# Twenty-eight weight tiles of a hybrid decoder layer multiplied by seven block products for eight, in a stage of their own ahead of attention

## The reference, cut to what matters

```python
mod = silu(c) @ w_ada + b_ada                      # shift, scale, gate
h = rmsnorm(x, norm_w) * (1 + scale) + shift       # 1024 tokens x 1024 channels
aq, ak, av, az, mq, mk, mv, mo, mz, mi, mf, ga, gm = split(h @ w_in)
att = sliding_window_attention(rope(aq), rope(ak), av, sinks)
y_att = (att * silu(az)) @ w_att
mq = silu(causal_conv(mq)); mk = silu(causal_conv(mk)) * d ** -0.5
hm = mlstm_chunkwise(mq, mk, mv, mi + b_i, log_sigmoid(mf + b_f))   # 4 heads of 256
hm = hm * rsqrt(mean(hm * hm) + eps) * m_norm_w * sigmoid(mo)
y_m = (hm * silu(mz)) @ w_m
merged = sigmoid(ga) * y_att + sigmoid(gm) * y_m
out = rmsnorm(x + gate * (merged @ w_out), final_norm_w)
```

## Time and profile before

| | |
|---|---|
| time, median of 3 runs | 1346.77 us (1345.74 to 1346.91) |
| profiled execution, first to last instruction (its span; the profile states no other time of it) | 1343.5 us |
| PE busy | 1308.8 us, 97% |
| DVE, ACT, POOL busy | 644.1, 427.4, 609.3 us |
| chain that ended last | PE 92%, DVE 4%, ACT 2% |
| moved by DMA | 89.44 MB, mean 67 GB/s |

### The profile page before, as it was taken

One profiled execution on the slowest core, in us unless ns is written; L12 is line 12 of the kernel. 1 busy time (PEld: TensorE's weight loads), 2 busy tenths in 40 slices (PEclk: granted clock), 3 DMA queues, 4 the chain that ended last, 5 costly groups with the idle time before them and its releaser, 6 DMA issues.

```text
span 1343.5 us, 20127 instructions
## 1 busy us (share of the span) xinstructions
PE 1308.8 (97%) x6941; PEld 1112.3 (83%) x6941; DVE 644.1 (48%) x1343; ACT 427.4 (32%) x1065; POOL 609.3 (45%) x824
## 2 busy tenths in 40 slices
PE   4899999999999999999999999999999999999997
PEld 3687988889788888889888988898889888788886
DVE  5776775857750000354554355435544421544335
ACT  5556564554630000133313332323232211311111
POOL 3507052160634444592665176517660555567240
PEclk9899999999999999999999999999999999999999
DMA  9702011020211310420410041004100133331602
GB/s 327 194 17 64 17 48 33 1 63 0 56 49 54 94 48 30 126 64 1 110 47 16 0 109 47 16 0 119 53 16 16 47 110 94 110 94 47 204 26 100
DMA packets 124951, 89.44 MB, mean 67 GB/s; under 512 B 12370, under 2 KB 117986, under 8 KB 124899
## 3 DMA queue, kind: packets, MB, share of 16 engines
q1 hardware_dynamic: 121056, 76.09, 20.2%
q10 hardware_dynamic: 3842, 12.68, 2.8%
HBM read 80.36 MB, written 8.41 MB: 66 GB/s over the span
## 4 chain that ended last, share of the span: by engine, by line
PE 92%; DVE 4%; ACT 2%; issue 1%; DMA 1%; ACTq 0%; POOL 0%; DVEq 0%
PE pp L574 27%; PE pp L575 26%; PE pp L576 26%; PE pp L742 2%; PE pp L853 2%; PE pp L725 1%; PE pp L726 1%; PE pp L733 1%; PE pp L662 1%; PE pp L845 1%; PE pp L710 1%; DVE prob_t L1485 1%; PE pp L648 1%; DMA freq<-inv_freq 1%; DVE pp L1423 1%
## 5 line engine op out<-in xcount | busy, mean ns | idle before, releaser
L513 POOL TENSOR_TENSOR w_hi<-raw,ones 128x256 fp32r<-128x256 f32 x388 | 263.9, 710 | 614.0 <-ACTq L371 342.3
L574 PE MATMUL pp<-h_hi,w_hi 128*128 128x512 f32 x896 | 349.9, 391 | 0.1
L575 PE MATMUL pp<-h_lo,w_hi 128*128 128x512 f32 x896 | 349.0, 390 | 0.0
L576 PE MATMUL pp<-h_hi,w_lo 128*128 128x512 f32 x896 | 348.8, 389 | 0.0
L517 POOL TENSOR_TENSOR w_lo<-raw,w_hi 128x256 fp32r<-128x256 f32 x388 | 319.7, 854 | 7.6
L576 PEld LDWEIGHTS pp<-h_hi,w_lo 128*128 128x128 f32 x896 | 168.2, 188 | 35.3
L574 PEld LDWEIGHTS pp<-h_hi,w_hi 128*128 128x128 f32 x896 | 168.3, 188 | 34.7 <-issue 0.7
L575 PEld LDWEIGHTS pp<-h_lo,w_hi 128*128 128x128 f32 x896 | 168.3, 188 | 33.5
L574 PE MATMUL pp<-w_hi,h_hi 128*128 128x256 f32 (+2 forms) x496 | 154.8, 312 | 2.0 <-ACT v_tok L1049 1.2
L576 PE MATMUL pp<-w_hi,h_lo 128*128 128x256 f32 (+2 forms) x496 | 153.1, 309 | 0.0
L575 PE MATMUL pp<-w_lo,h_hi 128*128 128x256 f32 (+2 forms) x496 | 152.9, 308 | 0.0
(11 more groups left out here) (259 smaller groups left out, 1928.1 us busy)
## 6 DMA issues: line engine op xcount, KB each, us to landing
raw<-w_in SPq DMA_DIRECT2D x70, 512.0 KB, 3.9
w_mod<-w_ada SPq DMA_DIRECT2D x6, 1024.0 KB, 12.7
x_in<-x SPq DMA_DIRECT2D x4, 1024.0 KB, 10.0
raw<-w_att SPq DMA_DIRECT2D x8, 512.0 KB, 5.6
merged_dram<-mix_a ACTq DMA_DIRECT2D x8, 512.0 KB, 2.6
w_gate<-w_ada ACTq DMA_DIRECT2D x8, 512.0 KB, 3.6
raw<-w_m SPq DMA_DIRECT2D x8, 512.0 KB, 3.8
mix_in<-merged_dram ACTq DMA_DIRECT2D x8, 512.0 KB, 3.3
```

Source lines behind the costliest of these rows:

```text
L513: ins = pool.tensor_tensor(hi[:, q, :], raw[:, s, q, :], one[:, q, :], ALU.mult)
L574: pe.matmul(o, lh, rh, start=first, stop=False)
L575: pe.matmul(o, lh, rl, start=False, stop=False)
L576: return pe.matmul(o, ll, rh, start=False, stop=last)
```

## The change

28 of the 32 tiles of ga, gm, mo and mz leave their stages: ga 2 to 7, gm 0 to 5, all eight mo and all eight mz. They form 14 pairs (`GATE_PAIRS`), 3 of ga, 3 of gm, 8 of (mz t, mo t). A pair times h is a 2 by 2 block product (two tiles, two halves of the 1024 channels, two halves of the tokens), and Strassen's scheme in its Winograd form makes it with 7 block products for 8. One product is 4 kt by 3 passes: 12 matmuls of 512 columns. The sums of weight blocks are made by DVE (`sum_of`, 4 a pair), high parts of the 7 operands by ACT (`operand_high`), low parts by POOL (`operand_low`) into a ring of 10 (`RING`) laid over the slots' memory. Four sums of quarters of h are made once (`token_sum`, `token_high`, `token_low`) in the memory of x. DVE adds the product banks to blocks (`add_first`, `add_seventh`, `block_22`, `block_21`, `block_12`), ACT applies sigmoid or silu, DVE multiplies silu(mz), sigmoid(mo) and the norm weight, and SP stores the results to `sig_dram` and `gate_dram`; later stages load them back (`load_sig`, `gate_m`, `sig_m`).

The stage stands between the head of the kernel and A; products 0 and 1 (pairs 0 and 1, product 1) stand ahead of `mod_rows(3, 0)`. `first_two_units` is gone; the first two token blocks are ordinary units after the stage. 2 MB of pair tiles are loaded ahead of `w_mod` blocks 2 and 3; the q, k and v tiles come at the stage's end. In C the mz and mo units are gone: mv0 follows mk3, chunk(i, 7) and the turning of the heads move into the mq units of the next head, or D1 after the last. D1 keeps two gm tiles, in slots 0 and 1, and `y2_first` comes behind it; the gate sum moves into D2; D2's slots are now 2, 4, 0, 1, 2, 4, 0, 1. POOL's order for E is unchanged. Loops of PE, ACT and DVE over heads are written out; small copies of per-head columns go.

```diff
-SLOT_USES = {"A": (4,) * 5, "B": (4, 4, 4, 4, 0), "C": (8,) * 5,
-             "D1": (2, 2, 2, 0, 2), "D2": (2, 2, 2, 0, 2), "E": (1, 1, 1, 1, 0), "E2": (1, 1, 1, 1, 0)}
-D_SLOTS = (0, 1, 2, 4)
+SLOT_USES = {"A": (4,) * 5, "B": (3, 3, 2, 2, 0), "C": (4, 4, 8, 4, 4),
+             "D1": (1, 1, 0, 0, 0), "D2": (2, 2, 2, 0, 2), "E": (1, 1, 1, 1, 0), "E2": (1, 1, 1, 1, 0)}
+D1_SLOTS = (0, 1)
+D_SLOTS = (2, 4, 0, 1)
...
+C_UNITS = [("mq", n) for n in range(4)] + [("mk", n) for n in range(4)] + [("mv", n) for n in range(NB)]
...
+GATE_PAIRS = [("a", 2), ("a", 4), ("a", 6), ("m", 0), ("m", 2), ("m", 4)] + [("o", t) for t in range(KT)]
+PRODUCTS = (1, 6, 7, 5, 2, 4, 3)
+EARLY = [(p, prod) for prod in (1, 5, 2, 3, 7, 6, 4) for p in range(2)]
+G_ORDER = EARLY + [(p, prod) for p in range(2, NG) for prod in PRODUCTS]
...
             load_mod(0)
             load_mod(1)
+            for k in range(2):
+                for p in range(2):
+                    load_pair_slot(p, k)
             load_mod(2)
             load_mod(3)
...
+            for g in range(FIRST_OPS, len(G_ORDER)):
+                operand_low(g)
...
+            def product(g):
...
+                pe.wait_ge(op_ready, g + 1)
+                if p == 0 and kind == "t":
+                    pe.wait_ge(t_ready, T_ORDER[prod])
+                t = slice(th * HALF, (th + 1) * HALF)
+                for k in range(HK):
+                    kt = kh * HK + k
+                    if p == 0 and kind == "h":
+                        pe.wait_ge(h_lo_ready, kt + 1)
+                    pe.matmul(o, op_hi[:, slot, k, :], hi[:, kt, t], start=first and k == 0, stop=False, skip_group_check=True)
+                    pe.matmul(o, op_hi[:, slot, k, :], lo[:, kt, t], start=False, stop=False, skip_group_check=True)
+                    ins = pe.matmul(o, op_lo[:, slot, k, :], hi[:, kt, t], start=False, stop=k == HK - 1, skip_group_check=True)
+                ins.then_inc(product_made, 1)
...
             turn_mod(PAIRS - 1)
-            first_two_units()
+            for g in range(2, len(G_ORDER)):
+                product(g)
+            for s in range(3):
+                after(pe, slot_split[s], use("A", s, 1))
...
+            for k, s in enumerate(D1_SLOTS):
+                after(pe, slot_split[s], use("D1", s, 1))
+                for half in range(2):
+                    feature_unit("D1", 0, 0, 2 * k + half, s, half, h_hi, h_lo)
+                    if (k, half) == (0, 0):
+                        chunk(MH - 1, NB - 1)
+                    if (k, half) == (1, 0):
+                        turn_heads(MH - 1)
...
+                add_seventh(p)
+                block_22(p)
+                block_21(p)
+                if not last:
+                    sum_of(4, p + 1)
+                block_12(p)
 
             for s, raw_s in ((1, raw_q[:, :, 1, :]), (2, raw[:, 2, :, :])):
                 after(dve, slot_hi[s], use("A", s, 1))
```

More of the change, by code:

```diff
@@ L439, in _, with load_sig @@
-            with sp.Fori(0, MH, 1) as i:
+            def load_sig(j):
+                if j == 2:
+                    after(sp, att_gated, 2 * KVH)
+                else:
+                    sp.wait_ge(mix_moved[j % MIX_BUFS], 16 * (mix_moves(j) - 1))
+                sp.dma_start(mix[j % MIX_BUFS][:, :], sig_v[:, j, :]).then_inc(mix_moved[j % MIX_BUFS], 16)
+            for q in range(2):
+                sp.wait_ge(spilled[q], 16 * spills_before(NG + q))
+            for kind, j, s, k in B_TILES:
+                src = w_in_v[:, :, GA + j * P:GA + (j + 1) * P] if kind == "ga" else w_att_v[:, :, j * P:(j + 1) * P]
+                load(src, s, use("B", s, k))
+                if kind == "wa" and j in (5, 6):
+                    load_sig(j - 3)
@@ L455, in _ @@
-            with sp.Fori(0, 2, 1) as i:
-                for k, s in enumerate(D_SLOTS):
-                    src = w_m_v[:, :, bass.ds(sp.snap(k * P + i * 512), P)]
-                    load(src, s, use("D2", s, 0) + i)
-            sp.wait_ge(gate_bias_added, 1)
+                if i:
+                    after(sp, ym_ready, 4 * i)
+                else:
+                    after(sp, bank_full[0], unit("C", 8, 0, 0)[1] + 1)
+                sp.dma_start(gate_m[:, :, :], gate_v[:, 2 * i:2 * i + 2, :]).then_inc(gate_m_loaded, 16)
@@ L461, in _ @@
+            after(sp, gate_sum, KT + 1)
             for s in (3, 0, 1, 2):
@@ L556, in _ @@
                         ins.then_inc(mask_added, 1)
[L557 to L560 removed]
+            for s in D1_SLOTS:
+                split(s, use("D1", s, 0), loads("D1", s, 1))
+            with pool.Fori(0, 2, 1) as i:
+                for s in D_SLOTS:
+                    split(s, use("D2", s, 0) + i, loads("D2", s, 1) + i)
             for s in (3, 0, 1, 2):
@@ new lines, in gate_out @@
+            def gate_out(p, c):
+                q = p % 2
+                func = ACT.Silu if GATE_PAIRS[p][0] == "o" and c in ("c11", "c12") else ACT.Sigmoid
+                tile = stage[q][{"c11": "e1", "c12": "u2", "c21": "c21", "c22": "u3"}[c]]
+                if c == "c11":
+                    act.wait_ge(product_made, G_AT[p, 2] + 1)
+                    act.wait_ge(blocks_made, BLOCK_AT[p, "u2"] + 1)
+                else:
+                    act.wait_ge(blocks_made, BLOCK_AT[p, c] + 1)
+                act.activation(tile[:, :], bank(q) if c == "c11" else tile[:, :], func).then_inc(gates_made, 1)
@@ L1202, in _ @@
-                    if (kind, n) == ("mo", 0):
-                        after(act, h_norm_step, 3 * i + 1)
-                        act.activation(h_rms[:, :], h_ms[:, :], ACT.Sqrt).then_inc(h_rms_done, 1)
+                            decays(i, 2, NB)
+                        else:
+                            chunk_out(i, n - 1)
+            for k in range(2):
+                for half in range(2):
+                    b = full("D1", 0, 0, 2 * k + half)
+                    if half:
+                        free(act, D1_SLOTS[k])
+                    act.activation(sig_m[:, 6 + k, half * HALF:(half + 1) * HALF], bank(b), ACT.Sigmoid).then_inc(bank_free[b], 1)
+                    if (k, half) == (0, 0):
+                        head_end(MH - 1)
```

873 lines of the change are left out of this document (579 added, 294 removed).

## The result

The changed kernel takes 1368.43 us (median of 4 runs, 1366.8 to 1370.53) beside 1346.26 us for the kernel before: a ratio of 1.0166, 95% interval 1.0151 to 1.018. It is slower, and 8 us slower than the 1360.2 us of the forecast, inside its range of 1347 to 1375. Its profiled span is 1366.7 us, 23.2 more than the 1343.5 of before.

The account below looks back on a forecast made before the run. The kernel was taken as bound by PE's number of matmuls. Stops and clock of +51.7 us less 38.3 for removed matmuls gave +13.4: span 1356.9, plus 3.3 to the median, 1360.2 us (chance 0.62), range 1347 to 1375.

Parts of the forecast that it names:

- C: Four heads: without mz0 ahead of mv0, PE waits for mk_t, +5.1 us a head, +20.4 us, bounds 19 and 23.
- D1: Ahead of D1: its first gm unit waits for POOL's split of slot 0, freed late by mv7; +3.0 us.
- the stage to attention: After the last product: w0's low parts stand behind block_12 in DVE's queue; +3.7 us, bounds 3.4 and 6.
- E: Ahead of E: last w_m tile in slot 1 leaves two POOL splits behind D2's end; +9.9 us, bounds 9.2 and 11.
- clock: PE's granted clock falls after long waits: three losses of 1.9 us taken, +5.7 us, bounds 0 and 12.
- head: Kernel start through the fourteen early products: late w_mod and product 6's wait; +4.5 us, bounds -5 and +9.
- D1 to D2: y2_first behind the last sigmoid, and 16 low parts, not 12, plus a memset; +4.5 us, bounds 3 and 5.5.
- Every stop costs the clock: Rival, whole kernel: six stops at 1.9 us, some twice that, +12 for +5.7; 1366.5 us, chance 0.14.
- product 6 waits for DVE, ACT and POOL in a row, about 3 us: In the head, behind h's last low part near 62 us: product 6 waits about 3 us for its operands.
- some 325: Start of A's first unit after the stage, in us, from 57 - 2 + 268.5 + 3.7.
- The rival in which POOL paces the whole stage: In the stage: low parts at 1.56 us an instruction make a pair 21.8 us; 1391 us, chance 0.06.
- The removed work: On PE: 168 fewer matmuls (1344 to 1176) at 0.228 us, worth 38.3 us.

Follow-up runs that it names:

- e5: e1 plus two tiles for E loaded ahead of the gate's sum and POOL splitting in order 2, 0, 3, 1; 1356.03 us, ratio 1.0076.
- e8: Changed kernel with the edits of e4, e5, e6 and e7 together; 1336.46 us, ratio 0.9925 to the kernel before.
- e9: e8 with C's value units one chunk earlier and ACT's v high part, y2_first and high parts of products 8 and 9 moved earlier; 1320.08 us, ratio 0.9806.
- e2: Changed kernel with 115 unread matmuls filling PE's stops ahead of turn_k of chunk 0 (four heads) and ahead of E; 1360.96 us, ratio 1.0115.
- e7: Changed kernel with product 3's weight sums and high parts ahead of product 7's token steps, and w0's low parts ahead of the last block_12; 1362.6 us, ratio 1.0125.
- e6: Changed kernel with each head's last convolution (mk1) and its SiLU made in two halves of 512 tokens; 1353.96 us, ratio 1.0054.
- e10: Changed kernel with DVE's low parts of three token sums replaced by one-input scaled copies, low parts left out of the result; 1366.34 us, one execution.
- e1: Changed kernel with w_m tiles in slots 2, 0, 1, 4 and loads and splits for E in order 3, 2, 0, 1; 1360.74 us, ratio 1.0113.
- e12: Changed kernel with POOL making each low part of a product's weights in one 512-column instruction instead of two of 256; 1364.33 us, ratio 1.0137.
- e4: e1 plus D1's two gate tiles in slots 3 and 4 in place of 0 and 1; 1359.97 us, ratio 1.0108.

## Why the prediction was right, and where it was not

*Direction, place and kind of the stops: right.* Every large stop is where the prediction put it, behind the work that it named. C (18.8 for 20.4), D1 (3.0 for 3.0), the stage to attention (3.4 for 3.7) and E (10.3 for 9.9) were read from rows of the kernel before by asking what the removed unit had covered and what is late next. e5 takes E's away and gives 12.4 us, for 10.3 of stop and 2.5 of clock. e8 had 10.3 us of stops and 6.8 of clock left in C; e9 takes them away, with two small edits elsewhere, and is 16.4 us under it. The total is nearer than its terms: clock and head had 15 us too little, and C, D1 to D2 and the stage to attention 5 too much. The direction did not hang on that.

*The clock: mis-sized, 16.7 for 5.7.* The term "I take three such losses" took the one loss of before (1.9 us behind 4.45 us) and counted it for a few stops, since nothing showed whether a stop amid dense work does the same. It does: from product 6 on every stop of 3.8 us and more did it, in all kernels here, and those of 5 us in C were worth up to 2.8 us each. "Every stop costs the clock" was the right rival, with 1366.5 us for 1368.4. The Trainium skill's rule ("TensorE: Matmul & The Clock Gate", "HAM oscillation"), that idle gaps inside a kernel throttle the array again each time, agrees with e2, where filling stops and nothing else gave 7.5 us. It did not hold for all short ones (lengths are gaps between matmuls, 0.15 us more than the waits): the stop of 2.3 us at D2 cost it in one of eleven profiles; of 15 stops of 2.4 to 3.0 us in C, D1 and D2 nine did, and of the six ahead of products 8 and 9 in e7, e8 and e9 the three second ones; of ten of 3.4 to 3.7 us eight did. The same stop at D1 did in e2, e6 and e10 and not in the changed kernel, e1, e5, e7 and e12, so the length alone does not settle it. Nor does the kernel: four executions of the changed kernel had mean granted clocks of 0.979 to 0.983 and lay 3.7 us apart, where one stretch of 3.4 us at the lower level is worth 0.001 of the mean and 1.7 us. Each kernel has one profile, so these counts are of single executions, and what decides a short stop stays open.

*The head: mis-sized, 8.6 for 4.5.* `w_mod` was late by 3.3 us, as worked out. The term that was mis-sized is "product 6 waits for DVE, ACT and POOL in a row, about 3 us": it waited 6.6. The row with POOL's 1.17 us an instruction had stood beside DVE instructions of 1024 columns, and I used it beside ones of 2048, where POOL takes 2.8. The Trainium skill ("SBUF — State Buffer", "SBUF: two separate sides") has the pair of ports held for the whole instruction; with POOL at 2.79 beside DVE's 2.82 the trace agrees. Two instructions at 2.17 and 2.77 in place of 1.17 are 2.6 us more, and the head's sum would have been 7.1. The other 1.5 us are not taken apart; the low clock behind `w_mod` is in them. The first unit of A began at 333.00. The prediction has "some 325", but its own terms add up to 327.2. The rival in which POOL paces the whole stage was wrong: inside it DVE's instructions are 512 columns (0.69 us), and POOL's mean over all is 0.874.

*D1 to D2: the size was wrong, 1.4 for 4.5.* I had used 0.85 us for a low part, from 10.23 us for twelve. After, the first four take 2.50 and the next twelve 7.25 us, 0.6 each: POOL's split, which ran beside the first of them before (1158.49 to 1165.84), is not there now. And before had lost 1.4 us of its own in the same place. That `y2_first` behind the last sigmoid was the cause is borne out by e9, where it stands ahead and 0.57 us are left.

*The removed work: right.* In e9, with the stops gone, 25.8 of the 38.3 us are there. Most of the rest is the head, which even in e9 is some 10 us behind the kernel before.

## What to carry to other kernels

Where PE is the bound, work that is taken away was also somebody's cover. For each unit that goes or moves, ask what was being made behind it and which queue makes it; here 38 us of matmuls uncovered 45 us of stops, and the stops took another 17 by the clock. The stops and their clock cost more than the arithmetic saved, and most of them were orders that could be turned: slot numbers, the order of splits, a load behind an unrelated wait, the order of a queue, and in C one convolution cut in two. Where VectorE and POOL both read SBUF side by side, price POOL's instruction at no less than the length of VectorE's, expect VectorE's to grow by most of what POOL's takes alone, and give POOL few long ones: that brought 4 us in e12.

## What the runs showed of the hardware that I had not expected

- POOL's 256-column instruction takes 0.73 us alone, 2.79 beside a 2048-column instruction of DVE with two inputs (2.82) and 1.71 beside one with a single input (1.75).
- It works the other way too. DVE's 2048 columns with two inputs take 2.28 us alone, 2.82 beside POOL's instructions of 256 columns and up to 3.38 beside those of 512 (e12). A tap of the convolution of 512 columns took 0.78 us alone and 1.04 beside POOL's splits (e6), three of 1024 columns 3.92 and 4.84 us (e4).
- 115 matmuls whose result nobody reads made the kernel 7.5 us faster (e2). They stood in stops, where PE had nothing else to do.
- Whether a stop of 2.4 to 3.7 us lowers the clock changed between kernels in which the stop is the same, and by the mean clocks between executions of one kernel. Comparing two versions by a few us can turn on this: at the stop ahead of attention, 3.27 us long in both, e4's profiled execution was at the lower clock for 6.8 us and e1's for 3.4.
